# Opening of a two-block transformer kernel: the input is also laid out by feature and loaded straight to its place, the token rows come behind it, and the row scale moves to the end of the first group

## The reference

```python
def rms_norm(x, w):
    xf = x.astype(jnp.float32)
    y = xf * lax.rsqrt(jnp.mean(xf * xf, axis=-1, keepdims=True) + EPS)
    return (y * w.astype(jnp.float32)).astype(x.dtype)

# mixer_block(u = rms_norm(x, norm_mix_w), ...)
z = u @ w_in            # (256, 2048) @ (2048, 11264)
```

## Time and profile before

| what | us |
|---|---|
| median of 3 runs | 1898.34 (1896.65 to 1899.03) |
| the profiled execution, its time | 1896.75 |
| its span | 1895.0 |
| TensorE busy | 1879.0 (99%) |
| VectorE busy | 1102.0 (58%) |
| ScalarE busy | 888.9 (47%) |
| mean rate of the DMAs | 183 GB/s |

### The profile page before, as it was taken

How to read it: one execution, slowest core, us unless ns; L and a number is a source line. 1 busy time by engine, 2 the same in 40 slices (tenths; PEclk the granted TensorE clock), 3 DMA queues, 4 the chain that set the end, 5 groups by cost and what they waited for, 6 DMA issues and landing times.

```text
span 1895.0 us, 33988 instructions
## 1 busy us (share of the span) xinstructions
PE 1879.0 (99%) x13480; PEld 1744.6 (92%) x13480; DVE 1102.0 (58%) x1278; ACT 888.9 (47%) x1171; POOL 143.3 (8%) x122
## 2 busy tenths in 40 slices
PE   8999999999999999999999999999999999999998
PEld 8989998999999989988998899899889998899986
DVE  6546766667655555545445445445565556867664
ACT  6534444465544445443444344334454355664443
POOL 2001322411001100000010000000010000000000
PEclk9999999999999999999999999999999999999999
DMA  8666566566565656656665665566556665354454
GB/s 272 180 181 176 183 178 178 156 203 184 170 229 192 211 189 178 193 199 192 195 192 193 193 192 195 191 190 188 189 188 179 178 172 151 102 152 136 156 191 142
DMA packets 176435, 346.49 MB, mean 183 GB/s; under 512 B 10976, under 2 KB 11184, under 8 KB 175776
## 3 DMA queue, kind: packets, MB, share of 16 engines
q1 hardware_dynamic: 174176, 337.76, 57.3%
q0 software_dynamic: 2128, 6.82, 1.4%
HBM read 342.44 MB, written 2.10 MB: 182 GB/s over the span
## 4 chain that ended last, share of the span: by engine, by line
PE 97%; DVE 2%; ACT 0%; DMA 0%; issue 0%; SPq 0%; DVEq 0%; ACTq 0%
PE ps L440 58%; PE ps L452 33%; PE ps L778 1%; PE ps L542 1%; DVE wlo L1278 1%; PE ps L742 1%; PE ps L765 0%; ACT whi L882 0%; DMA raw<-in_w_in_dram 0%; PE ps L470 0%; PE ps L753 0%; PE ps L593 0%; PE ps L585 0%; DVE xlo L1300 0%; PE ps L604 0%
## 5 line engine op out<-in xcount | busy, mean ns | idle before, releaser
L1278 DVE TENSOR_TENSOR wlo<-raw,whi 128x1024 fp32r<-128x1024 f32 x631 | 796.6, 1269 | 699.5 <-ACT whi L882 698.6
L882 ACT ACTIVATE whi<-raw 128x1024 fp32r<-128x1024 f32 x631 | 664.7, 1059 | 888.0 <-PE ps L440 556.4
L440 PE MATMUL ps<-xhi,whi 128*128 128x256 f32 (+1 forms) x1904 | 542.6, 285 | 0.6 <-DVE wlo L1278 0.5
L440 PE MATMUL ps<-xhi,wlo 128*128 128x256 f32 (+1 forms) x1904 | 531.7, 279 | 0.0
L440 PE MATMUL ps<-xlo,whi 128*128 128x256 f32 x1664 | 462.8, 278 | 0.0
L440 PEld LDWEIGHTS ps<-xhi,whi 128*128 128x128 f32 x1904 | 359.5, 189 | 9.5 <-issue 6.9
L440 PEld LDWEIGHTS ps<-xhi,wlo 128*128 128x128 f32 x1904 | 357.8, 188 | 0.0
L440 PEld LDWEIGHTS ps<-xlo,whi 128*128 128x128 f32 x1664 | 313.4, 188 | 1.5 <-issue 0.7
L440 PE MATMUL ps<-x2hi,whi 128*128 128x256 f32 x1024 | 283.0, 276 | 0.0
L440 PE MATMUL ps<-x2hi,wlo 128*128 128x256 f32 x1024 | 282.9, 276 | 0.0
L440 PE MATMUL ps<-x2lo,whi 128*128 128x256 f32 x1024 | 282.9, 276 | 0.0
(11 more groups left out here) (367 smaller groups left out, 2377.3 us busy)
## 6 DMA issues: line engine op xcount, KB each, us to landing
raw<-in_w_in_dram SPq DMA_DIRECT2D x279, 512.0 KB, 3.8
raw<-in_w_up_dram SPq DMA_DIRECT2D x128, 512.0 KB, 3.7
raw<-in_w_down_dram SPq DMA_DIRECT2D x128, 512.0 KB, 3.8
raw<-in_w_out_dram SPq DMA_DIRECT2D x64, 512.0 KB, 3.8
raw<-in_w_branch_a_dram SPq DMA_DIRECT2D x16, 512.0 KB, 4.8
raw<-in_w_branch_b_dram SPq DMA_DIRECT2D x16, 512.0 KB, 4.1
x_nat<-in_x_dram SPq DMA_DIRECT2D x4, 512.0 KB, 7.2
rel<-in_rel_turned_dram POOLq DMA_DIRECT2D x8, 256.0 KB, 4.5
```

The costliest lines, as they stand in the source:

```text
L440: ins = mm(outs[b], w[:, k % SLOTS, j, cols], v, start=start, stop=last and j == CK - 1 and i == 2, skip_group_check=True)
L882: f(whi[:, k % SLOTS], raw[:, k % SLOTS], ACT.Copy).then_inc(whi_ready, 1)
L1278: tt(wlo[:, k % SLOTS], raw[:, k % SLOTS], whi[:, k % SLOTS], ALU.subtract).then_inc(wlo_ready, 1)
```

## The change

The host also lays x out by feature, `x_turned`, 128 partitions by 16 tiles by 256 tokens, and `norm_mix_w` by feature. SP loads five pieces of it (2, 2, 4, 4 and 4 tiles) into `xt`, and `mix_w` to its place; ACT and DVE read `xt` where they read PSUM before. The transposes of x and of the norm's weights go; `warm` is now 16 matmuls of ones. The token rows `x_nat`, still needed for the squares, are loaded behind. The last four pairs of tiles are split in the loop over chunks, each pair with its chunk; the squares follow the splits of chunks 6 to 9, the scale is computed behind the split of chunk 10, and `row_scale` comes behind chunk 7 on PE. Less the plain renamings:

```diff
+XT_PIECES = ((0, 2), (2, 4), (4, 8), (8, 12), (12, KT))
@@ sync
-            sp.dma_start(ident[:], identity).then_inc(ident_in, 16)
-            sp.dma_start(mix_rows[:], norm_mix_w[0].rearrange("(k p) -> k p", p=P)).then_inc(mix_in, 16)
-            for c in range(4):
+            def turned_rows(c):
+                lo, hi = XT_PIECES[c]
+                sp.dma_start(xt[:, lo:hi, :], x_turned[:, lo:hi, :]).then_inc(xt_in[c], 16)
+            def token_rows(c):
                 cols = slice(c * CW, (c + 1) * CW)
                 sp.dma_start(x_nat[:, :, cols], x[0, :, cols].rearrange("(t p) d -> p t d", p=P)).then_inc(x_in[c], 16)
...
+            turned_rows(0)
+            sp.dma_start(mix_w[:], norm_mix_w).then_inc(mix_in, 16)
+            first = rows(w_in_t, 0, slice(0, CW))
+            sp.dma_start(raw[:, 0, 0], first[:, 0]).then_inc(half_in, 16)
+            sp.dma_start(raw[:, 0, 1], first[:, 1]).then_inc(raw_in[0], 16)
+            for c in range(1, 4):
+                turned_rows(c)
+                chunk(C_IN, c, rows(w_in_t, c, slice(0, CW)))
+                if c == 1:
+                    sp.dma_start(ident[:], identity).then_inc(ident_in, 16)
+            turned_rows(4)
+            token_rows(0)
+            token_rows(1)
             for k in range(4, NC):
                 chunk(C_IN, k, rows(w_in_t, k, slice(0, CW)))
+                if k < 6:
+                    token_rows(k - 2)
@@ tensor
-            def turn_start(c):
...
             def warm(n):
+                pe.wait_ge(ones_set, 1)
                 for i in range(n):
-                    nc.tensor.transpose(ps[:, 2, 0:P], ident[:], ident[:])
+                    mm(ps[:, 2, 0:P], ones[:], ones[:], start=True, stop=True)
...
                         if k == 0:
-                            warm(11)
-                            turn_start(0)
-                            warm(9)
-                        if k < 3:
-                            turn_start(k + 1)
+                            warm(16)
                         if k == 3:
                             turn_vectors()
-                        if k == 6:
-                            row_scale()
                         pe.wait_ge(x_ready, CK * (k + 1))
...
+                    if k == NC - 1 and g == 0:
+                        row_scale()
@@ scalar
             def start_upper(kt):
-                act.wait_ge(n_tr, kt // 2 + 1)
-                f(uhi[:, kt, :], ps[:, 4 + (kt % 8) // 2, (kt % 2) * T:(kt % 2) * T + T], ACT.Copy,
-                  scale=mix_w[:, kt:kt + 1]).then_inc(n_hi, 1)
+                act.wait_ge(xt_in[piece_of(kt)], 16)
+                f(uhi[:, kt, :], xt[:, kt, :], ACT.Copy, scale=mix_w[:, kt:kt + 1]).then_inc(n_hi, 1)
...
+                    if g == 0 and k < 4:
+                        for kt in (2 * (LEAD + k), 2 * (LEAD + k) + 1):
+                            start_upper(kt)
                     split_hi(C_IN + NC * g, LEAD + k)
-                    if g == 0 and k == 1:
+                    if g == 0 and 2 <= k < 6:
+                        start_squares(k - 2)
+                    if g == 0 and k == 6:
                         act.wait_ge(n_sum, 1)
                         f(ss[:, 0:2], ss[:, 0:2], ACT.Sqrt, bias=eps_t[:], scale=1.0 / D).then_inc(n_sd, 1)
@@ vector (start_lower, start_rows alike)
-                if k == 1:
+                if k == 6:
                     dve.wait_ge(n_sd, 1)
+                    dve.wait_ge(ident_in, 16)
                     nc.vector.reciprocal(rstd[:, 0:2], ss[:, 0:2]).then_inc(n_rs, 1)
...
-                if k == 6:
+                if k == NC - 1:
                     dve.wait_ge(m_row, 1)
                     own(nc.vector.tensor_copy(row_m[:], ps[:, 4, 0:T]))
@@ host
+              "x_turned": laid["x"][0].T.reshape(KT, P, T).transpose(1, 0, 2)}
+    laid["norm_mix_w"] = inputs["norm_mix_w"].reshape(KT, P).T
```

More of the change, by code:

```diff
@@ L98, in unit_at, with piece_of @@
     return None
+def piece_of(kt):
+    return [lo <= kt < hi for lo, hi in XT_PIECES].index(True)
 def pair_at(at):
@@ L109, in program @@
             k_norm_g_2, lambda_q1_2, lambda_k1_2, lambda_q2_2, lambda_k2_2, subln_g_2, w_out_2,
-            post_norm_g_2, identity, level_masks, rope_cos, rope_sin, rope_turn, distance, rel_turned, triangles, out):
+            post_norm_g_2, identity, level_masks, rope_cos, rope_sin, rope_turn, distance, rel_turned, x_turned, triangles, out):
     with ExitStack() as ctx:
@@ L208, in program @@
         x2lo = at("x2lo", 64, [P, KT, T], F32R)
-        mix_rows = at("mix_rows", 56, [KT, P])
+        xt = at("xt", 0, [P, KT, T])
         diag_m = at("diag_m", 60, [P, NT, P])
@@ L252, in program @@
         x_in = [sem(f"x_in{c}") for c in range(4)]
+        xt_in = [sem(f"xt_in{c}") for c in range(len(XT_PIECES))]
         half_in, half_hi, half_lo = [sem(n) for n in ("half_in", "half_hi", "half_lo")]
@@ L919, in start_squares @@
                 square(0, c, x_nat[:, 0, cols], junk[:, cols], 0, n_ss)
-            act.wait_ge(mix_ready, 1)
+            act.wait_ge(mix_in, 16)
             for k in range(LEAD):
-                for kt in (2 * k, 2 * k + 1) if k < 2 else range(4 * k - 4, 4 * k):
+                for kt in (2 * k, 2 * k + 1):
                     start_upper(kt)
@@ L930, in _ @@
                     split_hi(C_IN, k)
[L931 to L934, removed]
             def start_meta():
@@ L1304, in _ @@
             nc.vector.memset(eps_t[:], EPS).then_inc(setup, 1)
-            own(nc.vector.memset(ones[:], 1.0))
+            nc.vector.memset(ones[:], 1.0).then_inc(ones_set, 1)
             def start_squares(c):
@@ L1311, in start_squares @@
                                                ALU.mult, ALU.add, accum_out=sq[:, 0, 1, c:c + 1]).then_inc(n_ss, 1)
-            dve.wait_ge(mix_t, 1)
-            nc.vector.tensor_copy(mix_w[:], ps[:, 3, 0:KT]).then_inc(mix_ready, 1)
-            dve.wait_ge(mix_ready, 1)
+            dve.wait_ge(mix_in, 16)
             for k in range(LEAD):
-                for kt in (2 * k, 2 * k + 1) if k < 2 else range(4 * k - 4, 4 * k):
+                for kt in (2 * k, 2 * k + 1):
                     start_lower(kt)
@@ L1324, in _ @@
                     split_lo(C_IN, k)
-                    start_squares(k - 1)
-            for kt in range(12, KT):
-                start_lower(kt)
-            start_squares(3)
             def start_rows(k):
-                if k == 0:
+                if 2 <= k < 6:
+                    start_squares(k - 2)
+                if k == 5:
                     dve.wait_ge(n_ss, 8)
                     nc.vector.tensor_reduce(ss[:, 0:2], sq[:, 0], AX.X, ALU.add).then_inc(n_sum, 1)
-                if k == 1:
+                if k == 6:
                     dve.wait_ge(n_sd, 1)
+                    dve.wait_ge(ident_in, 16)
                     nc.vector.reciprocal(rstd[:, 0:2], ss[:, 0:2]).then_inc(n_rs, 1)
@@ L1503, in _ @@
                 for k in range(NC):
+                    if g == 0 and k < 4:
+                        for kt in (2 * (LEAD + k), 2 * (LEAD + k) + 1):
+                            start_lower(kt)
                     split_lo(C_IN + NC * g, LEAD + k)
@@ L2011 @@
     laid["x"] = laid["x"][:, places]
-    turned = {"rel_turned": inputs["rel_bias"][:, :, ::-1]}
+    turned = {"rel_turned": inputs["rel_bias"][:, :, ::-1],
+              "x_turned": laid["x"][0].T.reshape(KT, P, T).transpose(1, 0, 2)}
+    laid["norm_mix_w"] = inputs["norm_mix_w"].reshape(KT, P).T
     for name, a in [*laid.items(), *constants.items(), *turned.items(), *last.items()]:
```

16 lines of the change are left out of this document (6 added, 10 removed).

## The result

The changed kernel takes 1900.22 us (median of 12 runs) and the kernel before 1897.37 us (12 runs on the same chip). The ratio is 1.0016, with a 95% interval of 1.0009 to 1.0024. That is 2.9 us slower, and the interval leaves no change out. The prediction had 1898.1 us, 0.2 us faster. The time lies in the predicted range and within 0.2% of before, but the sign is wrong, and by its own steps chunk 8 should have started at 35.6 us and started at 38.85. (One of the 12 runs was disturbed, at 2336 us, and is left out of the ratio; without it the median is 1900.15.)

A forecast was written before the change was run, and what follows sets the result against it. TensorE was taken as the bound (busy 1879.0 of 1895.0 us), with saturated DMAs in the opening. The gain of 3.3 us at chunk 0 shrinks to 1.7 at chunk 4 and 0.2 at chunk 8: 1898.1 us, range 1894.5 to 1901.0.

The forecast's parts named there:

- Start of chunk 0: Opening on TensorE: first x landed at 4.2, ScalarE from 4.3, chunk 0 at 6.9 us, 3.3 us earlier.
- Landing times: Opening loads: 2.81 us per MB queued; chunk 1 lands at 8.0, chunk 4 at 20.0, chunk 6 at 25.9 us.
- Row scale: Behind chunk 7: chunk 10's landing at 32.3 gates it, second diagonal at 35.2, TensorE waits 1.3 us.
- rival E: Ahead of chunk 4: TensorE's clock falls after the idle, costing 1.2 us, 1899.1 us; chance 0.10.
- rival B: From chunk 8: the wait before the row scale makes the fast matmul pace hold, saving 2.3 us, 1895.8 us; chance 0.19.
- The mark: Start of chunk 8, 35.77 us before: total time moves as much as it does, unless matmul pace changes; 35.6 forecast.
- rival D: Opening: loads keep up, chunks 0 to 7 run without a wait, chunk 8 5.3 us earlier, 1892.8 us; chance 0.06.

The follow-up runs named there:

- e3: Changed kernel without the 8 instructions squaring the token rows (sums set to a constant), rows still loaded: 1897.28 us, ratio 1.0004 to before.
- e1: Changed kernel with the row scale on TensorE one chunk later, behind chunk 8: 1899.11 us, ratio 1.0015 to before.
- e5: Kernel before with only the row scale moved behind chunk 7 on TensorE and its copy behind the split of chunk 11: 1896.67 us, ratio 0.9999.
- e9: Kernel before with 2 MB of unused token rows loaded behind chunks 1, 2 and 3: 1899.7 us, ratio 1.0017.
- e8: Changed kernel with token rows loaded behind chunk 7, and squares, scale and evacuation of group 0 in group 1: 1900.14 us, ratio 1.0018 to before.
- e4: Changed kernel without squares of the token rows and without loading those rows (2 MB): 1893.92 us, ratio 0.9984 to before.
- e2: Changed kernel with 11 unused float32 products ahead of the row scale to fill TensorE's wait: 1899.44 us, ratio 1.0015 to before.
- e12: Changed kernel without token rows; ScalarE and VectorE square the laid-out x, TensorE sums over features: 1895.54 us, ratio 0.9994 to before.
- e10: Changed kernel without token rows; GpSimd squares the laid-out x and adds its tiles, TensorE sums over features: 1905.9 us, ratio 1.0046 to before.
- e6: Changed kernel with the norm's weights set to ones instead of loaded in 64-byte rows: 1899.59 us, ratio 1.0014 to before.

## Why the prediction was wrong

**Start of chunk 0: right.** 6.9 us predicted, 6.90 measured, with a little luck: ScalarE began at 3.95, not 4.3, and the first half of `wlo` was done at 6.6, but `warm` ran until 6.90 and not 6.5. The 0.2 us vanish in the next wait.

**Landing times: too early by 1.6 us.** The line through two loads of before, 2.81 us per MB, was used for a queue that begins otherwise. Chunk 1 was there at 9.58 (8.0 predicted), chunk 4 at 21.75 (20.0). The offset arises before chunk 1 and stays between 1.0 and 1.7 us up to chunk 6 (27.11, predicted 25.9), so the slope was right and the intercept wrong. It goes with the gap from 5 to 7 us, whose cause is open. So chunk 4 gave back all of the 3.3 us, and the 1.7 us that should have been left were not.

**Row scale: the step that failed.** "Work on DVE and ACT is only shifted, not added" is true of its amount, but the amount now has to be done between the late landing of chunk 4 and the request at 35.35. The prediction took chunk 10's landing as the gate, with 1.3 us of waiting. Chunk 10 was in time; 10.1 us of VectorE's work in a row were the gate, and the wait was 3.03. The second diagonal was ready at 38.33 and not at 35.2, 3.1 us late. Had chunk 6 landed at the predicted 25.9, the same row of work would have ended near 25.9 + 1.1 + 10.1 = 37.1 (an estimate), still 1.9 us late; the other 1.2 are the late landing of chunk 6. e3 bears it out: without the squares 0.60 of the wait are left. I should have laid VectorE's own instructions end to end from the landing of chunk 4, as I did for TensorE's.

**The clock: rival E, given 0.10, came true at other places.** It fell behind the waits before chunk 1 and before the row scale, not before chunk 4. The price of 1.2 us was nearly right (1.5). The first was absorbed: chunk 4 was waiting for its load anyway, and e1, whose clock did not fall before it, stood there for 2.92 us in place of 1.80. The second carried to 66.00.

**The pace: rival B's mechanism came, and decides nothing.** TensorE in the changed kernel:

```profile
65.00:85.00 20.00, 20.00 (x183) 1.00 0.70 209
185.00:205.00 20.00, 20.00 (x178) 1.00 0.50 155
```

The 183 can't be set against the 173 of the earlier trace rows, since it takes in the 16 short turns of the meta tokens. The distance between matmuls can: around 70 us it is 0.113 us in the changed kernel and 0.118 in the kernel before. The second mark is the first `kr` product behind these groups, first before, then changed:

```profile
132.91 0.83 PE L536 MATMUL ps<-qp,kr 128*128 128x128 f32 x6
```

```profile
135.48 0.72 PE L540 MATMUL ps<-qp,kr 128*128 128x128 f32 x5
```

From the turn of the meta tokens that is 71.60 us before and 69.48 changed, so the changed kernel won back 2.1 us. But e5 and e9, which are the kernel before in this stretch, also took 69.5 us, and their medians are that of before and 2.9 us more. The pace changes from run to run, and from one profile it can't be credited to a kernel. About 2 us at the end of the changed kernel's profile are of this kind as well: from the last idle of TensorE (1781.73, before 1778.54) to the end of the span it took 118.7 us against 116.5, and e9 took 118.4.

**The mark.** That the time moves as much as the start of chunk 8 looks right for the changed kernel (3.1 and 2.9 us), and is in part luck, as a clock loss of 1.6 us behind the mark stands against the pace. For other kernels it fails: e1 has the mark of before (35.90) and is 2.3 us slower, e8 reaches it 3.8 us early and is 3.6 us slower. The waits and the clock behind the mark count too.

**The direction of the argument was right, its size not.** The prediction had the loads eat the gain down to nothing. They ate more: 2 MB more cost 2.9 us even with nothing else changed (e9), and without them, and the squares that hang on them, the changed opening is 2.9 us faster than before (e4). What the runs show is that the second reading of x, in a stretch in which the DMAs have no room, costs as much as the change saves at its start, and that the squares push it over: e3, with the second reading and without the squares, is not measurably slower than before. e1, e2 and e8 move or fill the wait and leave the time about where it is. How the 2.9 us split between late splits, VectorE's backlog and the clock is not settled: the medians resolve about 1.7 us. (A slip of the prediction without consequence: rival D's 5.3 us count from the kernel before and were taken off the forecast; 1893.0 us is meant.)

## What to carry to other kernels

Where the opening is bound by loads, count the bytes first: a layout that saves work on TensorE but reads the same data twice pays for it in the chunks behind, and here moving the wait mostly changed its place. When a late load pushes work together, add up the queue of each engine behind that load, not only the next load. And if an input is wanted in two layouts, look for a way to compute from the one already there, as e12 does.

## What the runs showed of the hardware

- GpSimd's multiplications of 128x1024 and its addition of 128x2048 float32 (1.9 to 4.6 us each) stretched VectorE's pairs of 128x256 from 0.87 us to 3.96 and 6.81 us (e10).
- The granted clock fell to 1.2 GHz behind idles of 1.83 (e2), 1.94 (e4), 2.16, 2.92 (e1) and 3.03 us, and did not behind 1.80 (changed kernel, chunk 4), 1.74 (e1), 2.07 (e6) and 2.35 (e2). The length of one idle did not tell it. The Trainium skill, "TensorE: Matmul & The Clock Gate", Part 1, says that the array falls back after idling; the trace agrees for the waits around 3 us, and the 1.83 that fell beside the 2.35 that did not is left open.
- Many of SyncE's issues of 0.4 us took longer once much was queued (1.06 us at 5.04, 1.40 at 9.51 and 2.19 at 12.40 in the changed kernel; 0.98 at 6.23 in e9, where the kernel before stays at 0.55 or less up to 5.8 us), and delayed what is issued next. Those of chunks 4 and 5 between them took 0.38 and 0.37, so what sets it is not shown.
- The same 256-column matmuls follow each other every 0.113 or every 0.118 us at a granted clock of 1.00, and which of the two differs between profiles of the same code (e5 and e9 against before, 50 to 130 us).
